# A hybrid GLA / SGU / cross-attention / MoE layer: x turned raw, its inverse root applied behind the projections, and the first weights loaded in quarters

## What is computed

```python
h = _rmsnorm(x, norm_mix_g)                    # x * rsqrt(mean(x*x) + EPS) * g
p = h @ w_in                                   # q, k, v, r, a_low, u, sv, gates
y_a = _gla(q, k, v, r, a_low, ...) @ w_proj_a  # gated linear attention, chunks of 64
y_b = _sgu(u, sv, ...) @ w_proj_b              # spatial gating
x = x + (sigmoid(g_a) * y_a + sigmoid(g_b) * y_b) @ w_mix_out
x = x + cross_attention(rmsnorm(x), rmsnorm(mem))
x = x + moe(rmsnorm(x))                        # 32 experts, top 4 of each token
out = rmsnorm(x)
```

## Time and profile before

| | |
|---|---|
| median of 3 runs | 1205.45 us (1203.64 to 1205.8) |
| the profiled execution | 1202.94 us, its span 1201.2 us |
| busy share of the span | PE 98%, PEld 45%, DVE 23%, ACT 24%, POOL 18% |
| DMA | 377 GB/s over the span, 427 GB/s from 297 to 600 us |

### The profile page before, as it was taken

How to read it: one execution, slowest core, us unless ns; L and a number is a source line. 1 busy time by engine, 2 the same in 40 slices (tenths; PEclk the granted TensorE clock), 3 DMA queues, 4 the chain that set the end, 5 groups by cost and what they waited for, 6 DMA issues and landing times.

```text
span 1201.2 us, 13973 instructions
## 1 busy us (share of the span) xinstructions
PE 1175.1 (98%) x5626; PEld 541.6 (45%) x5626; DVE 278.3 (23%) x588; ACT 282.4 (24%) x412; POOL 211.1 (18%) x68
## 2 busy tenths in 40 slices
PE   9999999999999999999999999999999999999996
PEld 8888898987333333333333333333333333333332
DVE  2862255034111111211121111111122111111112
ACT  6654445462111111111111111111111111111112
POOL 8976898830000000000000000000000000000000
PEclk9999999999999999999999999999999999999999
DMA  9744765729999999999999999999999999999996
GB/s 344 277 161 150 270 246 173 280 114 395 420 428 429 428 427 428 428 429 429 428 428 428 429 428 428 430 429 428 428 429 428 428 428 428 429 428 430 428 427 265
DMA packets 55770, 453.17 MB, mean 377 GB/s; under 512 B 7030, under 2 KB 7612, under 8 KB 30012
## 3 DMA queue, kind: packets, MB, share of 16 engines
q1 hardware_dynamic: 55376, 452.20, 91.1%
q10 hardware_dynamic: 364, 0.54, 0.1%
HBM read 451.68 MB, written 1.05 MB: 377 GB/s over the span
## 4 chain that ended last, share of the span: by engine, by line
PE 84%; DVE 6%; DMA 4%; ACT 2%; issue 2%; SPq 2%; DVEq 0%; POOL 0%; ACTq 0%; POOLq 0%
PE ps L1841 30%; PE ps L1889 18%; PE ps L1406 13%; PE ps L1809 4%; DMA late<-in_w_e 4%; PE ps L1450 4%; PE ps L1742 2%; PE ps L1873 2%; PE ps L1609 2%; DVE shared L1315 2%; DVE shared L1307 2%; PE ps L1820 2%; DVE shared L1327 2%; ACT shared L835 2%; PE ps L1783 1%
## 5 line engine op out<-in xcount | busy, mean ns | idle before, releaser
L1841 PE MATMUL ps<-late,shared 128*64 128x512 f32 x1024 | 226.2, 594 | 0.7 <-DMA late<-in_w_e 0.6
L526 POOL TENSOR_TENSOR pairs<-raw,pairs 128x2048 fp32r<-128x2048 f32 x42 | 197.8, 4721 | 60.5 <-ACT pairs L613 60.4
L1307 DVE TENSOR_SCALAR shared<-ps 128x512 f32<-128x512 f32 x32 | 22.1, 692 | 530.7 <-PE ps L1841 530.7
L1841 PEld LDWEIGHTS ps<-late,shared 128*64 128x64 f32 x1024 | 71.9, 137 | 150.5 <-issue 147.5
L1406 PE MATMUL ps<-pairs,hT 128*128 128x512 f32 x576 | 133.6, 391 | 0.0
L835 ACT ACTIVATE shared<-shared 128x512 f32<-128x512 f32 x32 | 20.2, 631 | 469.0 <-DVE shared L1307 469.0
L1406 PEld LDWEIGHTS ps<-pairs,hT 128*128 128x128 f32 x576 | 107.4, 188 | 22.7 <-issue 0.7
L613 ACT ACTIVATE pairs<-raw 128x2048 fp32r<-128x2048 f32 x42 | 80.4, 1918 | 60.3 <-PE ps L1406 34.1
L847 ACT ACTIVATE shared<-ps 128x512 f32<-128x512 f32 x32 | 19.1, 598 | 205.3 <-PE ps L1889 205.3
L1742 PE MATMUL ps<-normed,shared 128*64 128x512 f32 x248 | 66.9, 618 | 0.0
L1809 PE MATMUL ps<-shared 64*128 64x512 f32 x256 | 63.6, 615 | 0.7 <-ACT shared L847 0.7
(11 more groups left out here) (232 smaller groups left out, 1018.4 us busy)
## 6 DMA issues: line engine op xcount, KB each, us to landing
late<-in_w_e SPq DMA_DIRECT2D x78, 2048.0 KB, 30.7
raw<-in_w_e SPq DMA_DIRECT2D x31, 2048.0 KB, 31.3
shared<-in_w_e SPq DMA_DIRECT2D x30, 2048.0 KB, 30.3
free_slot<-in_w_e SPq DMA_DIRECT2D x15, 2048.0 KB, 30.5
extra<-in_w_e SPq DMA_DIRECT2D x15, 2048.0 KB, 31.4
after_rows<-in_w_e SPq DMA_DIRECT2D x14, 2048.0 KB, 31.3
raw<-in_w_in SPq DMA_DIRECT2D x18, 1024.0 KB, 6.0
raw<-in_w_xk SPq DMA_DIRECT2D x4, 1024.0 KB, 6.3
```

The lines of the kernel that those rows point to most:

```text
L526: g.tensor_tensor(low, raw_half(m), high, ALU.subtract).then_inc(s["low_made"], 1)
L1307: V.tensor_scalar(glu, ps[:, HIDDEN_BANKS[0], :], LIMIT, None, ALU.min).then_inc(s["glu_made"], 1)
L1841: last = M.matmul(ps[64 * j:64 * j + 64, HIDDEN_BANKS[h], :], xeT[:, c % 2 * W1_SUB + part, j0:j0 + SLOTS], w[:, h * D + j * HALF:h * D + ...
```

## The change

x is turned by plain transposes as each tile lands. The gain is applied as before; the inverse root is applied behind the products: as a scale of ACT's copies and functions for v, r, sv, u and the gates, by DVE for `aL`, q and k with a matrix `rstd_rows` that holds the root of each token along the columns in every partition. PE makes that matrix as a new group `rB`, the product of ones and the two diagonals, between qk and `aL`. The first weight half comes in two quarters, each split by ACT on its own; the first pass of q and k runs over the first quarter, then over the second. The small vectors come in two tiles (`vec_rows` for the first gain, `more_rows` for the others, in the slot of a later weight chunk), each turned in a group of its own, so `GROUPS` gains `more_vecs` and `rB`. Both squares of x are ACT's. High parts of xT00 and xT10 are made first on DVE, then the low ones, then the diagonals. Six small loads move behind weight half 5. The third and fourth half are split by ACT ahead of `mem`'s squares. 20 idle products become 7 and 4. Some semaphores are merged.

```diff
-FIRST_IDLE_PRODUCTS = 20
+FIRST_IDLE_PRODUCTS = 7
+WEIGHTS_IDLE_PRODUCTS = 4
...
-GROUPS = (["vecs"] + each("xT") + ["aL", "q", "k", "la", "v0", ...
+GROUPS = (["vecs"] + each("xT") + ["more_vecs", "aL", "q", "k", "rB", "la", "v0", ...
...
-            load_half(0)
+            src, _ = piece_source("qk")
+            for q in range(2):
+                sp.dma_start(raw_half(0)[:, q * D:(q + 1) * D].rearrange("p (c n) -> p c n", c=2),
+                             src[:, 2 * q:2 * q + 2, :]).then_inc(raw_full[0] if q else s["first_quarter_in"], 16)
             load_half(1)
...
             for n in range(N_RAW_SLOTS, HALVES):
+                if n == 2 * PIECES.index("sv"):
+                    small_loads()
                 if n == 2 * PIECES.index("ga0"):
+                    filled(sp, "more_vecs")
                     load_chunk(0, 0, True)
...
-            sc.wait_ge(s["x_in0"], 16)
-            A.activation(normed[:, 0, :], rows[:, 0, :], ACT.Square, accum_out=stat[:, N_X + 4:N_X + 5]).then_inc(
-                s["x_sq"], 1)
+            for t in range(TT):
+                sc.wait_ge(s[f"x_in{t}"], 16)
+                A.activation(normed[:, t, :], rows[:, t, :], ACT.Square,
+                             accum_out=stat[:, N_X + 4 + t:N_X + 5 + t]).then_inc(s["x_sq"], 1)
             sc.wait_ge(s["ident_made"], 3)
             root(stat[:, N_X + 4:N_X + 6], stat[:, N_X + 4:N_X + 6], D, "x_sq", 2, "x_std")
-            high_parts("qk", 0)
+            for q in range(2):
+                cols = slice(q * D, (q + 1) * D)
+                sc.wait_ge(raw_full[0] if q else s["first_quarter_in"], 16)
+                A.activation(pair(0)[:, 0].rearrange("p c n -> p (c n)")[:, cols], raw_half(0)[:, cols], ACT.Copy).then_inc(
+                    s["high_made"] if q else s["first_quarter_made"], 1)
+            split[0] = 1
             emptied(sc, "vecs")
-            high_scaled("xT", 1, 0, hT, G_MIX)
             high_scaled("xT", 0, 1, hT, G_MIX)
             high_scaled("xT", 1, 1, hT, G_MIX)
-            high_parts("v", 0)
+            high_parts("v", 1)
...
+            filled(ve, "vecs")
+            V.tensor_copy(vecs[:, 0:8], bank("vecs")[:, 0:8]).then_inc(bank_emptied[bank_of("vecs")], 1)
+            emptied(ve, "vecs")
+            for t in range(TT):
+                high_T("xT", t, 0, hT, G_MIX)
+            low_T("xT", 0, 0, hT, G_MIX)
+            low_T("xT", 1, 0, hT, G_MIX)
+            filled(ve, "more_vecs")
+            V.tensor_copy(vecs[:, 8:38], bank("more_vecs")[:, 0:30]).then_inc(bank_emptied[bank_of("more_vecs")], 1)
+            low_T("xT", 0, 1, hT, G_MIX)
+            low_T("xT", 1, 1, hT, G_MIX)
             inv(N_X + 4, 2, "x_std", "x_rstd")
...
+            filled(ve, "rB")
+            V.tensor_copy(rstd_rows, bank("rB")[:, 0:T]).then_inc(bank_emptied[bank_of("rB")], 1)
+            emptied(ve, "rB")
             filled(ve, "aL")
-            V.tensor_copy(aT[:], bank("aL")[0:2 * RANK, 0:T]).then_inc(bank_emptied[bank_of("aL")], 1)
+            V.tensor_tensor(aT[:], bank("aL")[0:2 * RANK, 0:T], rstd_rows[0:2 * RANK, :], ALU.mult).then_inc(
+                bank_emptied[bank_of("aL")], 1)
...
-            V.scalar_tensor_tensor(q_in, bank("q").rearrange("p (a b) -> p a b", a=2), GLA_DK ** -0.5, ec,
+            both = rstd_rows.unsqueeze(1).to_broadcast([P, 2, T])
+            V.tensor_tensor(q_in, ec, both, ALU.mult).then_inc(s["rstd_applied"], 1)
+            filled(ve, "k")
+            V.tensor_tensor(k_out, bank("k").rearrange("p (a b) -> p a b", a=2), both, ALU.mult).then_inc(
+                s["rstd_applied"], 1)
+            ve.wait_ge(s["rstd_applied"], 1)
+            V.scalar_tensor_tensor(q_in, bank("q").rearrange("p (a b) -> p a b", a=2), GLA_DK ** -0.5, q_in,
                                    ALU.mult, ALU.mult).then_inc(bank_emptied[bank_of("q")], 1)
-            filled(ve, "k")
+            ve.wait_ge(s["rstd_applied"], 2)
...
-                V.tensor_tensor(kz[p0:p0 + 64, h, :], bank("k")[p0:p0 + 64, f * T:(f + 1) * T], z[p0:p0 + 64, f, :],
-                                ALU.mult).then_inc(s["keys_made"], 1)
+                V.tensor_tensor(kz[p0:p0 + 64, h, :], k_out[p0:p0 + 64, f, :], z[p0:p0 + 64, f, :], ALU.mult).then_inc(s["keys_made"], 1)
...
-            V.tensor_tensor(k_out, bank("k").rearrange("p (a b) -> p a b", a=2), lns, ALU.mult).then_inc(
+            V.tensor_tensor(k_out, k_out, lns, ALU.mult).then_inc(
                 bank_emptied[bank_of("k")], 1)
...
-                        last = M.matmul(bank(f"xT{t}{k}")[:, i * P:(i + 1) * P], rows[:, t, c], normed[:, t, 0:P],
-                                        start=True, stop=True)
-                    end_group(last, f"xT{t}{k}")
+                    pe.wait_ge(s[f"x_in{t}"], 16)
+                    transposes(f"xT{t}{k}", [(rows[:, t, c * P:(c + 1) * P], P) for c in range(4 * k, 4 * k + 4)])
...
+            pe.wait_ge(s["consts_made"], 1)
+            start_group("rB")
+            for t in range(TT):
+                pe.wait_ge(s["diag_made"], t + 1)
+                last = M.matmul(bank("rB")[:, t * P:(t + 1) * P], ones[:], normed[:, t, 0:P], start=t == 0, stop=True,
+                                skip_group_check=True)
+            end_group(last, "rB")
             pe.wait_ge(s["wa_split"], 2)
             start_group("aL")
```

More of the change, by code:

```diff
@@ L93, in each @@
     return [prefix + g for g in TN]
-GROUPS = (["vecs"] + each("xT") + ["aL", "q", "k", "la", "v0", "v1", "r0", "r1", "sv0", "sv1", "wsT", "u0", "u1",
+GROUPS = (["vecs"] + each("xT") + ["more_vecs", "aL", "q", "k", "rB", "la", "v0", "v1", "r0", "r1", "sv0", "sv1", "wsT", "u0", "u1",
                                    "att0", "att1", "koT"] + each("memT")
@@ L674, in _ @@
                 filled(sc, f"r{t}")
-                A.activation(gate_r[:, t, :], bank(f"r{t}"), ACT.Sigmoid).then_inc(s["r_sig"], 1)
+                A.activation(gate_r[:, t, :], bank(f"r{t}"), ACT.Sigmoid, scale=x_rstd(t)).then_inc(s["r_sig"], 1)
             for n, dst, following in (("sv", sgu_v, "u"), ("u", sgu_u, "ga0")):
@@ L679, in _ @@
                     filled(sc, f"{n}{t}")
-                    A.activation(dst[:, t, :], bank(f"{n}{t}"), ACT.Gelu).then_inc(bank_emptied[bank_of(f"{n}{t}")], 1)
+                    A.activation(dst[:, t, :], bank(f"{n}{t}"), ACT.Gelu, scale=x_rstd(t)).then_inc(
+                        bank_emptied[bank_of(f"{n}{t}")], 1)
             high_parts("ga1", 0)
@@ L691, in gates_of @@
                     filled(sc, group)
-                    A.activation(dst[:, t, n * HALF:(n + 1) * HALF], bank(group), ACT.Sigmoid).then_inc(
+                    A.activation(dst[:, t, n * HALF:(n + 1) * HALF], bank(group), ACT.Sigmoid, scale=x_rstd(t)).then_inc(
                         bank_emptied[bank_of(group)], 1)
@@ L921, in low_of, with high_T, low_T @@
                                 ALU.subtract).then_inc(bank_emptied[bank_of(group)], 1)
-            def scaled_T(prefix, t, k, dst, gain):
+            def high_T(prefix, t, k, dst, gain):
+                group = f"{prefix}{t}{k}"
+                filled(ve, group)
+                V.tensor_tensor(dst[:, 0, 4 * k:4 * k + 4, t * P:(t + 1) * P], bank(group).rearrange("p (c r) -> p c r", c=4),
+                                vecs[:, gain + 4 * k:gain + 4 * k + 4].unsqueeze(2).to_broadcast([P, 4, P]),
+                                ALU.mult).then_inc(s["high_by_vector"], 1)
+            def low_T(prefix, t, k, dst, gain):
                 group = f"{prefix}{t}{k}"
@@ L948, in _ @@
             for t in range(TT):
-                V.tensor_scalar(normed[:, t, 0:P], ident[:], stat[:, N_X + 4 + t:N_X + 5 + t], None, ALU.mult).then_inc(
-                    s["diag_made"], 1)
-            filled(ve, "vecs")
-            V.tensor_copy(vecs[:], bank("vecs")[:, 0:38]).then_inc(bank_emptied[bank_of("vecs")], 1)
-            emptied(ve, "vecs")
-            for k in range(2):
-                for t in range(TT):
-                    scaled_T("xT", t, k, hT, G_MIX)
+                V.tensor_scalar(normed[:, t, 0:P], ident[:], x_rstd(t), None, ALU.mult).then_inc(s["diag_made"], 1)
             ve.wait_ge(s["wa_in"], 16)
@@ L1495, in _ @@
                         has_half("qk", half)
[L1496 to L1506 removed]
+                    if half + a + b == 0:
+                        start_group("q")
+                        start_group("k")
+                        todo = [(n, i, 2 * q + c) for q in range(2) for n in range(2) for i in range(2) for c in range(2)]
+                    else:
+                        todo = [(n, i, c) for n in range(2) for i in range(2) for c in range(DC // 2)]
+                    for n, i, c in todo:
+                        group, f = "qk"[n], 2 * n + i
+                        if half + a + b == 0 and (n, i, c) == (0, 0, 2):
+                            pe.wait_ge(s["high_made"], 1)
+                        last = M.matmul(bank(group)[:, i * T:(i + 1) * T], w[:, b, c, f * P:(f + 1) * P],
```

(3 more changed lines are left out.)

104 lines of the change are left out of this document (50 added, 54 removed).

## The result

The changed kernel takes 1220.78 us (median of 4 runs, 1219.35 to 1222.16) where the kernel before takes 1205.62 beside it (1203.64 to 1205.93): 1.0132 times the time before, 95% interval 1.0120 to 1.0145. That is 15.2 us slower, against 7.4 forecast, and above the end of the range. The profiled execution took 1219.98 us, its span is 1218.3, 17.1 longer than that of before. That is more than the 15.2 of the medians, because the profiled execution of before was 2.7 us under the 1205.62 here and that of after 0.8 under its own median.

What follows compares the result with a forecast made beforehand. PE order bounds the kernel until the attention ends, then the weight stream. 1.1 us of gain against about 7.9 of waits gives +6.8, plus 0.6 clock: 7.4 on the median 1205.45, so 1212.8; range 1208 to 1219.

Steps and rivals of the forecast that it cites:

- the step it rested on: At sv0 and sv1: they now wait for q's and k's banks, emptied by a longer chain that POOL holds; +6.8 us net.
- the rest: Ahead of sv1: what remains of about 7.9 us of PE waits after the 3.2 us ahead of sv0.
- rival A: Opening: POOL also gets between diagonals, cast and subtraction, so PE waits at `aL`; 1214 to 1219, chance 0.25.
- about 0.8 of DVE work that holds it off: Opening: DVE work keeps POOL out behind its first low part (14.44), before POOL's second and third parts.
- just in time: At `aL`: low half of v ready at 24.4, `aL` ending at 24.5 instead of 25.61.
- its far end: Rival A with POOL taking a turn after each step: `wa` split at 29, `aL` waits 6.5 us, end about +13.5.
- the clock: PE slow after the sv waits: 0.6 us taken, between nothing and about 3.3 us.
- the opening: PE from its start to `aL`: pass three 1.6 us earlier, less 0.46 for `rB`, gain 1.1 us.
- B: `kz` and k_out: chain not stopped by POOL, k emptied by 50.2, sum -0.6 us (1204.9), without any wait 1204.3; chance 0.10.

Runs made afterwards that it cites:

- the kernel with the diagonals on ACT: Changed kernel with the two diagonals made by ACT and the inverse root taken on DVE ahead of the vectors' second copy: 1213.12 us, 1.0078 times before.
- u's split early: Changed kernel with q and k emptied early, diagonals on ACT, first low part in quarters, u's second half split ahead of ACT's exponential: 1211.02 us.
- the filled waits: Changed kernel with idle products on PE in its waits, 26 ahead of `aL`: 1218.03 us; with 13 more ahead of each of sv0 and sv1: 1216.57 us.
- early emptying with ACT diagonals: Changed kernel with q and k multiplied by the root straight from PSUM behind `aL`'s copy, and both diagonals made by ACT: 1206.42 us, 1.0017 times before.
- rB first: Changed kernel with `rB` moved ahead of `aL` in the list of groups, so sv1 and `wsT` reuse q's and k's banks: 1214.14 us.
- one diagonal step: Changed kernel with both diagonals made in one DVE instruction in place of two: 1214.08 us, 1.0088 times before.

## Where the prediction was right and where it failed

**Right: the direction, and the step it rested on.** From the end of `aL` to the start of sv1 the forecast counted 58.1 - 24.5 = 33.6 us; in after it is 65.97 - 32.37 = 33.6. Ahead of sv0 it gave a wait of 3.2 (3.08), ahead of sv1 "the rest" of 7.9, that is 4.7: measured 2.89, with the 1.85 us by which sv0's products were slow in the same place. In the gate chain, ec times the root stood until POOL's part ended (52.59 + 4.57 = 57.16; POOL 52.02 + 4.59 = 56.61), q and k times the root took 0.68 each from PSUM, the first `kz` ended with POOL's next part. Pass three began within 0.1 us of the end of POOL's first part, as forecast (15.15 and 15.10). That nothing gives the time back held too. The kernel with the diagonals on ACT is the one that the forecast described, with no wait at `aL`: there `aL` ends at 24.85 (forecast 24.5) and sv1 starts at 58.46 (58.1). It is 9.2 us over the before beside it, and 7.4 of the forecast, 0.35 of lateness at `aL` and 1.2 more of clock behind sv1 make 9.0.

**Failed: the choice between the forecast and rival A.** The step was the "about 0.8 of DVE work that holds it off": I let the two diagonals, the cast and the subtraction keep POOL out together behind its first part, which puts the split of `wa` at about 14.44 + 0.8 = 15.2 and leaves no wait for it at `aL` (the "just in time" at 24.4 was the low half of v). I did so on the evidence of the earlier trace rows, and against the two scans with a POOL part between them, gave rival A 0.25 and left its far end out of the range. All four steps were held, `wa` was split at 28.86 (A's far end said 29), and `aL` waited 5.38 us (6.5 there). The rule of the Trainium skill that stood beside rival A (SBUF — State Buffer, Who interferes with whom) agrees with the trace of after: the second diagonal, an SBUF-only tensor-scalar, stood 4.67 us. The row at 82.40 showed POOL losing its turn where it came while DVE's steps were running; it did not show that POOL loses it where its next part is ready when its last one ends. Steps on SBUF were held in three more places: 7.74 and 5.58 us in the kernel with u's split early, 10.80 for its four `kz`.

**Failed in size: the clock.** The prediction had one term for it, 0.6 us, bounded by 3.3. Behind the two sv waits, for which it stood, 1.8 was paid (behind sv1; at sv0 nothing, as the filled waits show), three times the 0.6 but inside the bound. The other 1.6 came behind the wait at `aL`, which the forecast did not have. "PE works densely before the first wait" was no reason: 19 us at a granted clock of 1.00 stand before the wait at sv0, and the stretch behind it reads 0.63. The Trainium skill (TensorE: Matmul & The Clock Gate, What's actually happening) says that the throttled state is the default; the granted clock, which did not show a fall in the rows of before, reads 0.55 to 0.63 behind the three waits of after.

**Mis-sized: the opening.** PE's gain at pass three was to be 1.6 us and is 16.07 - 15.10 = 1.0. The second quarter landed at 9.34, not at 8.78, and its split took 1.06, not 0.96, so POOL began at 10.51 instead of 9.83. With 0.45 for `rB` and 64 passes in 7.93 us for 7.67, 0.16 is left (early emptying with ACT diagonals: `aL` ends at 25.45 for 25.61) where the prediction had 1.1. Together: 5.4 + 1.6 at `aL`, 0.9 in the opening and 1.2 more clock at sv1 are 9.1, and with the forecast's 7.4 that is the 16.5 at `wsT`.

**Rivals.** B (the chain not stopped by POOL) is out by the rows of DVE. A is what happened, at its far end. Its total there was about +13.5 (the forecast's 7.4 and the 6.5 at `aL` make 13.9) against 16.5 at `wsT`: the wait at `aL` was 1.1 shorter, the clock cost 2.8 more than the 0.6, and the opening gave 0.9 less.

## What to carry to other kernels

When work is moved onto DVE beside a POOL that has parts queued, price each DVE step of the kinds that were held here (tensor-scalar, cast, tensor-tensor, scalar-tensor-tensor and scan, all operands in SBUF) at one whole POOL part, and count the steps: joining two of them, giving them to ACT, or reading from PSUM took whole turns away here. A new PSUM group in a rotating list is a change of who waits for whom for everything behind it; write down the new pairs before counting what the group itself costs. And after a repair follow the moved work of the helper engine to its next meeting, not only to the wait that was removed.

## What the runs showed of the hardware

- Three 128x128 DVE steps on SBUF stood 4.5 to 4.7 us each, one after the other, beside a POOL that never paused; the cast took 0.60 in before, where POOL's part ended 0.52 us after its start, and the subtraction 0.29 in POOL's gap. Steps with an operand in PSUM (0.41, 0.68) were not held, nor were two kinds that read SBUF: a reciprocal of 128x2 (0.16, at 13.56 in after) and the statistics of 128x512 (0.64).
- In the first 100 us of these kernels PE fell to the 1.2 GHz level behind its longest waits (2.89, 2.90, 3.08, 5.37, 5.38 and 6.72 us, in all kernels that have them), and kept 2.4 GHz where such waits were filled with idle products. Behind the shorter ones the runs differ: waits of 2.26 (three kernels) and 1.75 us left the rate alone, one of 1.95 (rB first, granted clock 0.71 and 0.82 behind it) cost 1.6 us. Behind one of 2.01 (one diagonal step) PE ran at full rate, although the 12 products ahead of that wait had run at 0.50 throughout. What decides there was not settled.
